# Query projection fed by activations ahead of their normalisation, in a one-layer hybrid decoder step

## The reference, cut to what matters

```python
def rmsnorm(x, g):
    xf = x.astype(F32)
    y = xf * lax.rsqrt(jnp.mean(jnp.square(xf), axis=-1, keepdims=True) + NORM_EPS)
    return (y * g.astype(F32)).astype(x.dtype)

def mem_attn(h, mk, mv, w_mq, w_mo):
    q = (h @ w_mq).reshape(B, T, MEM_HEADS, MEM_HEAD_DIM)
    s = jnp.einsum('bthd,bmhd->bhtm', q, mk) * (MEM_HEAD_DIM ** -0.5)
    p = jax.nn.softmax(s, axis=-1)
    o = jnp.einsum('bhtm,bmhd->bthd', p, mv).reshape(B, T, D_MODEL)
    return o.astype(h.dtype) @ w_mo

    # in layer():
    x = x + jnp.concatenate([a, b], axis=-1).astype(x.dtype) @ w_out
    x = x + mem_attn(rmsnorm(x, norm_mem_g), mk, mv, w_mq, w_mo)
    x = x + peer(rmsnorm(x, norm_ffn_g), peer_wq, peer_subkeys, peer_u, peer_v)
```

## Time and profile before

| what | value |
|---|---|
| median of 3 runs | 4757.11 us (4755.58 to 4757.85) |
| the profiled execution | 4756.82 us, its span 4754.9 us |
| mean granted TensorE clock | 0.969 of full speed |
| PE busy | 4437.2 us, 93% |
| POOL busy | 3059.0 us, 64% |
| DVE busy | 2364.5 us, 50% |
| ACT busy | 1561.5 us, 33% |

### The profile page before, as it was taken

One profiled execution on the slowest core, in us unless ns is written; L12 is line 12 of the kernel. 1 busy time (PEld: TensorE's weight loads), 2 busy tenths in 40 slices (PEclk: granted clock), 3 DMA queues, 4 the chain that ended last, 5 costly groups with the idle time before them and its releaser, 6 DMA issues.

```text
span 4754.9 us, 75671 instructions
## 1 busy us (share of the span) xinstructions
PE 4437.2 (93%) x28747; PEld 4178.8 (88%) x28747; DVE 2364.5 (50%) x3080; ACT 1561.5 (33%) x1954; POOL 3059.0 (64%) x1558
## 2 busy tenths in 40 slices
PE   7999999898998989999999887999999999999997
PEld 7799999797887978888888787999999999999997
DVE  3622333313002165555555554666666666667656
ACT  4422222212222244444444443333333333333333
POOL 6833322232222457777777665899999899998864
PEclk9999999999998999999999888999999999999998
DMA  6643333423654255555555457899999999999964
GB/s 219 199 87 105 108 108 108 146 81 111 218 197 153 93 164 184 182 184 185 186 183 183 139 152 230 330 341 345 344 343 347 327 343 340 348 344 357 335 194 136
DMA packets 556785, 1031.87 MB, mean 217 GB/s; under 512 B 137073, under 2 KB 342001, under 8 KB 523889
## 3 DMA queue, kind: packets, MB, share of 16 engines
q1 hardware_dynamic: 314384, 590.67, 38.2%
q0 software_dynamic: 45056, 268.60, 14.4%
q10 hardware_dynamic: 197216, 170.85, 11.0%
HBM read 935.26 MB, written 94.73 MB: 217 GB/s over the span
## 4 chain that ended last, share of the span: by engine, by line
PE 37%; issue 26%; POOL 26%; DMA 4%; DVE 3%; another core or an unknown queue 2%; ACT 1%; ACTq 0%; POOLq 0%; DVEq 0%; SPq 0%
POOL WS L424 21%; PE PS L811 15%; PE PS L529 12%; PE PS L879 9%; POOL ROWS L458 3%; DMA AR<-in_vE 2%; POOL AR L448 2%; PE PS L854 1%; DMA RAW<-in_vE 1%; ACT WS L911 1%; DVE AR L1427 1%; DVE AR L1401 1%; DMA gel<-AR 0%; POOL AR L458 0%
## 5 line engine op out<-in xcount | busy, mean ns | idle before, releaser
L529 PE MATMUL PS<-HL,WS 128*128 128x288 f32 (+2 forms) x16896 | 2421.9, 304 | 122.1 <-DVE HL L1438 33.8
L529 PEld LDWEIGHTS PS<-HL,WS 128*128 128x128 f32 x16896 | 2367.5, 191 | 153.1 <-issue 102.4
L424 POOL TENSOR_TENSOR WS<-RAW,WS 128x1024 fp32r<-128x1024 f32 x602 | 1477.1, 2466 | 1296.0 <-ACT WS L911 1291.3
L879 PE MATMUL PS<-WW,WS 128*128 128x320 f32 x6144 | 940.8, 315 | 80.5 <-POOL WS L424 65.3
L879 PEld LDWEIGHTS PS<-WW,WS 128*128 128x128 f32 x6144 | 921.1, 192 | 99.5 <-issue 81.9
L911 ACT ACTIVATE WS<-RAW 128x1024 fp32r<-128x1024 f32 x602 | 617.8, 1055 | 994.9 <-PE PS L529 351.0
L811 PE MATMUL PS<-WS,HL 128*128 128x512 f32 x3072 | 700.1, 389 | 0.0
L811 PEld LDWEIGHTS PS<-WS,HL 128*128 128x128 f32 x3072 | 575.6, 188 | 118.9
L424 POOL TENSOR_TENSOR WS<-AR,WS 128x1024 fp32r<-128x1024 f32 x238 | 600.4, 2526 | 45.8 <-ACT WS L911 44.8
L424 POOL TENSOR_TENSOR WS<-CS,WS 128x1024 fp32r<-128x1024 f32 x200 | 492.5, 2462 | 199.7 <-ACT WS L911 198.1
L1714 DVE SCALAR_TENSOR_TENSOR PS<-ROWS,AR,PS 128x2048 f32<-128x2048 f32 x206 | 483.8, 2348 | 73.2 <-DMA ROWS<-in_vE,AR 72.9
(11 more groups left out here) (163 smaller groups left out, 2308.1 us busy)
## 6 DMA issues: line engine op xcount, KB each, us to landing
RAW<-in_uT SPq DMA_DIRECT2D x256, 512.0 KB
RAW<-in_w_lin SPq DMA_DIRECT2D x218, 512.0 KB
CS<-in_uT SPq DMA_DIRECT2D x128, 512.0 KB
AR<-in_uT SPq DMA_DIRECT2D x128, 512.0 KB
RAW<-in_vE SPq DMA_DIRECT2D x128, 512.0 KB
CS<-in_vE SPq DMA_DIRECT2D x64, 512.0 KB
AR<-in_vE SPq DMA_DIRECT2D x64, 512.0 KB
AR<-in_w_lin SPq DMA_DIRECT2D x46, 512.0 KB
```

Of the source, the lines that this page charges most:

```text
L424: pool.tensor_tensor(WS[:, k, 1, :], raw(k, many, late), WS[:, k, 0, :].bitcast(F32), ALU.subtract)\
L529: ins = mm(to, WS[:, slot + hf, wp, k * P:(k + 1) * P], x, start=first and (wp, xp) == (0, 0), stop=last and wp == 1, skip_group_check=True)
L879: ins = mm(bank(2 + d % 2, ND), WS[:, 2 * (q % 2) + b, vp, 512 * e + P * d4:512 * e + P * (d4 + 1)], W[:, 2 * b + e, wp, :], start=(b, e, ...
```

## The change

Three things are done.

1. The activations of the queries are split without the per-token factor: the high part is `X` times the gain, made by ACT in one instruction (L1192 of the new text), and the low part is `X` times gain minus the high part, in one DVE instruction (`gained_low`). Blocks 0 to 14 of `HL` are overwritten while PE works on output block 15, each as soon as PE has read the old block (`hl_free`). Block 15 follows when it has been added.
2. The sum of squares for the factor is taken by PE within `query(0, 0)`, after its tenth input block (`sum_within`). DVE makes the factor `RSTD`, and multiplies each query block by it when it takes it out of PSUM (`evac_queries`), for all four heads. ACT no longer evacuates queries. Queries are linear in the normalised activations, so the result is the same in exact arithmetic.
3. `X` is stored to `x2T` in four pieces, three of them during the output projection. SP loads the keys of head 0 after slice `H_MQ + 7` in place of `H_MQ + 11`, and waits for `RSTD` ahead of them. Buffers move to make room for `RSTD`.

```diff
-            load_lin(H_RET, H_MQ + 12)
+            load_lin(H_RET, H_MQ + 8)
             sp.wait_ge(S["lo_ready"], LO_MQ + 16)
-            sp.wait_ge(S["out_x"], 16)
+            sp.wait_ge(S["out_x"], 64)
+            sp.wait_ge(S["rstd_ready"], 1)
...
             load_keys(0)
+            load_lin(H_MQ + 8, H_MQ + 12)
...
                         if kb in marks:
                             ins.then_inc(S["used"], 1)
+                        elif frees:
+                            ins.then_inc(S[frees], 1)
...
-            norm_sum(2)
...
+            def sum_within(k2):
+                if k2 == 4:
+                    norm_sum(2)
             for m in range(4):
-                query(0, m)
+                query(0, m, sum_within if m == 0 else None)
...
-            add_stage(2, H_OUT, B_OUT)
-            act.dma_start(x2T.rearrange("k p t -> p k t"), X).then_inc(S["out_x"], 16)
+            for b in range(KB - 1):
+                act.wait_ge(S["used"], used(H_OUT + 2 * b + 2))
+                high2(H_OUT + 2 * b + 4, 2 * (b % 2))
+                if b:
+                    act.wait_ge(S["lin_evac"], B_OUT + b + 2)
+                    square(2, b - 1, X)
+                if b % 4 == 0 and b:
+                    act.dma_start(x2T[b - 4:b].rearrange("k p t -> p k t"), X[:, b - 4:b, :]).then_inc(S["out_x"], 16)
+            for b in range(KB):
+                if b == 7:
+                    act.wait_ge(S["used"], used(H_OUT + 2 * KB - 1))
+                elif b < KB - 1:
+                    act.wait_ge(S["hl_free"], b + (b < 7))
+                else:
+                    act.wait_ge(S["lin_evac"], B_OUT + KB + 2)
+                    square(2, KB - 1, X)
+                act.activation(HL[:, 0, b, :], X[:, b, :], ACT.Identity, scale=GAINS[:, G_MEM + b:G_MEM + b + 1])\
+                    .then_inc(S["hi_ready"], 1)
+                if b == 2:
+                    act.wait_ge(S["lin_evac"], B_OUT + KB + 1)
+                    square(2, KB - 2, X)
+            act.dma_start(x2T[KB - 4:KB].rearrange("k p t -> p k t"), X[:, KB - 4:KB, :]).then_inc(S["out_x"], 16)
+            act.wait_ge(S["used"], used(H_OUT + 2 * KB))
+            high2(H_OUT + 2 * KB + 2, 2)
             root(2)
-            for b in range(KB):
-                high_part(48, b)
...
-                copy(halves(QM[:, m, :]), pair(m % 2)).then_inc(S["lin_evac"], 1)
...
-            add_residual(2, H_OUT)
-            rstd(2, summed=True)
-            normed(X, G_MEM, LO_MQ)
+            def gained_low(b):
+                dve.wait_ge(S["hi_ready"], LO_MQ + b + 1)
+                stt(HL[:, 1, b, :], X[:, b, :], GAINS[:, G_MEM + b:G_MEM + b + 1], HL[:, 0, b, :].bitcast(F32),
+                    ALU.mult, ALU.subtract).then_inc(S["lo_ready"], 1)
+            for n in range(KB - 1):
+                add_block(2, H_OUT, n)
+                if n:
+                    add_square(2, n - 1)
+            for b in range(KB - 1):
+                gained_low(b)
+                if b == 2:
+                    add_square(2, KB - 2)
+            add_block(2, H_OUT, KB - 1)
+            add_square(2, KB - 1)
+            gained_low(KB - 1)
+            dve.wait_ge(S["sum_done"], 3)
+            ts(halves(NVAR), pair(3), EPS, None, ALU.add).then_inc(S["var_ready"], 1)
...
+            newton(NRS, NVAR, NACC, RSTD)
+            dve.sem_inc(S["rstd_ready"], 1)
             link(dve.memset(AR[:, 2304:3840], 0.0))
+            def evac_queries(h):
+                for m in range(4):
+                    dve.wait_ge(S["used"], h * 8 + used(H_MQ + 2 * m + 2))
+                    tt(halves(QM[:, m, :]), pair(m % 2), halves(RSTD), ALU.mult).then_inc(S["lin_evac"], 1)
+            evac_queries(0)
```

More of the change, by code:

```diff
@@ L239, in build @@
         INZ, OSR = ar(19408, 4, 32), ar(19536, RD)
[L241 to L244, removed]
+        QM, QZ, PTZ, RSTD = ar(0, 4, T), ar(2304, SB, 4, 32), ar(3328, 2, 2, 4, 32), ar(3840, T)
+        KT, VT, KVS = ar(4416, 4, MEM), ar(5440, 2, MD), ar(6464, SB, 2 * MD)
+        PR, PT, OB, OSB = ar(14656, TILES, MEM), ar(15936, 2, TP), ar(16960, 4, T), ar(14656, MD)
+        MX, NMX, SM, RSM = ar(19264, TILES), ar(19269, TILES), ar(19274, TILES), ar(19279, TILES)
         Z_OUT = (CS[:, 0, :], CS[:, 1, :], RAWQ[:, 4, :])
-        Z_MO = (CS[:, 0, :], CS[:, 1, :], ar(19220, T))
+        Z_MO = (CS[:, 0, :], CS[:, 1, :], ar(19284, T))
         QP, SC, SV = ar(0, 2, RT5), ar(1280, 2, TILES, NK), ar(2560, 2, TILES, TOPK)
@@ L507, in projection @@
             def projection(n, m, a, slot, moving=both_halves, ready=None, between=None,
-                           part=(0, KB), marks=(KB // 2 - 1, KB - 1), first_bank=None):
+                           part=(0, KB), marks=(KB // 2 - 1, KB - 1), first_bank=None, frees=None):
                 if part[0] == 0:
@@ L594, in out_early, with out_rest @@
                            marks=(KB // 2 - 1,) if m == 0 else (), between=between)
-            def out_rest(first, block, early, lo):
+            def out_rest(first, block, early, lo, frees=None):
                 for m, marks in ((0, (KB - 1,)), (1, (KB - 2, KB - 1))):
                     projection(first + 2 * m, block + m, m, 2 * m, ready=lo, part=(early, KB), marks=marks)
-                with pe.Fori(0, 7) as i:
+                with pe.Fori(0, 6) as i:
                     for s in range(2):
                         projection(i * 4 + (first + 4 + 2 * s), i * 2 + (block + 2 + s), s, 2 * s)
+                for b in (KB - 2, KB - 1):
+                    projection(first + 2 * b, block + b, b % 2, 2 * (b % 2), frees=frees if b == KB - 1 else None)
             def head_block(h, m, between=None):
@@ L715, in _, with query @@
             out_early(H_OUT, B_OUT, 1, OUT_EARLY, LO_OUT)
-            out_rest(H_OUT, B_OUT, OUT_EARLY, LO_OUT)
-            norm_sum(2)
-            def query(h, m):
-                projection(h * 8 + (H_MQ + 2 * m), h * 4 + (B_MQ + m), m % 2, 2 * (m % 2), ready=LO_MQ)
+            out_rest(H_OUT, B_OUT, OUT_EARLY, LO_OUT, frees="hl_free")
+            def query(h, m, between=None):
+                projection(h * 8 + (H_MQ + 2 * m), h * 4 + (B_MQ + m), m % 2, 2 * (m % 2), ready=LO_MQ, between=between)
             def attention(h, more):
@@ L1234, in _ @@
             for b in range(KB):
-                high_part_peer(64, b)
+                high_part_peer(48, b)
             act.wait_ge(S["lo_ready"], LO_FFN + 16)
@@ L1380, in _ @@
             for b, end in ((0, 4), (4, 8), (8, 12), (12, 14), (14, 16)):
-                act.wait_ge(S["t_ready"], 80 + end)
+                act.wait_ge(S["t_ready"], 64 + end)
                 act.dma_start(yT[b:end].rearrange("k p t -> p k t"), X[:, b:end, :]).then_inc(S["out_y"], 16)
@@ L1557, in _, with add_block @@
             dve.sem_inc(S["rvar_ready"], 1)
+            def add_block(k, first, n):
+                dve.wait_ge(S["used"], used(first + 2 * n + 2))
+                if n % 4 == 0:
+                    dve.wait_ge(S[f"in_x{n // 4}"], 16 * k)
+                tt(halves(X[:, n, :]), halves(X[:, n, :]), pair(n % 2), ALU.add).then_inc(S["lin_evac"], 1)
             def add_residual(k, first):
                 for n in range(KB):
[L1562 to L1565, removed]
+                    add_block(k, first, n)
                     if n:
@@ L1596, in attention @@
                 dve.sem_inc(S["p_done"], 1)
+                if more:
+                    evac_queries(h + 1)
             with step.loop(MH - 1, 3) as h:
```

15 lines of the change are left out of this document (8 added, 7 removed).

## The result

The changed kernel takes 4723.39 us (median of 4 runs, 4717.47 to 4724.72) against 4756.34 us of the kernel before (4 runs, 4755.15 to 4757.85). The ratio is 0.9928, its 95% interval 0.9911 to 0.9945, so it is faster by 26 to 42 us. 4725.8 was forecast.

What follows compares the result with a forecast made beforehand. PE was taken to bound the kernel, busy 93% of the span. Gains of 27.4 (pause) and 4.3 (keys) less 0.4 (evacuation) make 31.3 us, forecasting 4725.8 us; own range 4722 to 4729, range asked for 4720 to 4735.

Steps and rivals of the forecast that it cites:

- The pause: Between output block 15 and the end of the first query block: PE's idle and slow query go, 27.4 us gained.
- the tightest place: Norm's sum within the first query block: PE wants it at 1116.7, ready at 1116.9; 0.2 us of wait taken.
- The step that made the first low part late: During output block 15, POOL's weight work holds up DVE's first low part, which ends 0.6 us after POOL, at 1102.9.
- The value for the evacuation: DVE's evacuation of each head's fourth query block: 0.76 us against ACT's 0.65, 0.4 us lost over four heads.
- its upper bound of 2 us: If POOL holds up DVE's evacuations, up to 2 us for each of four, 8 us in all.
- The factor: Ahead of the first evacuation: ready at 1126.3, or about 1131 if POOL holds DVE up; needed at 1135.6, cost 0.
- The keys: Scores of head 0: earlier key loads remove PE's wait and slower matmuls around it, 4.28 us gained.
- A: DVE is held up in the first query block and at four evacuations; 10 us given back, about 4735; chance 0.10.
- C: The first query block cannot start until block 15's add; PE waits 9 us, 4735, or 4756 with whole pause; chance 0.03.
- B: The keys' gain in head 0 does not come; 4.3 us missing, 4730; chance 0.08.
- D: Slower: without the pause PE is granted less clock in the rest of the span; 4770 at 1% less; chance 0.03.
- the untouched stages: All behind the queries moves ahead as a whole; only the last head could shift by itself, 2 us either way.

Runs made afterwards that it cites:

- keys_only: The kernel before with only the keys of head 0 loaded after slice H_MQ + 7; 4688.9 us, ratio 0.9989.
- before_values_late: The kernel before, with the last head's cached values issued only when the 12 early low parts are made; 4680.78 us, ratio 0.9969.
- after_again: The changed kernel run again with no edit; 4662.88 us, ratio 0.9930 to the kernel before.
- after_third: The changed kernel run a third time with no edit; 4660.97 us, ratio 0.9926 to the kernel before.
- sum_at_once: The changed kernel with the norm's sum put back ahead of the first query block; 4674.64 us, ratio 0.9956 to the kernel before.
- split_after_block: The changed kernel with high and low parts made only after output block 15 has ended; 4667.7 us, ratio 0.9941 to the kernel before.
- keys_back: The changed kernel with the keys of head 0 loaded behind slice H_MQ + 11 again; 4665.7 us, ratio 0.9943 to the kernel before.
- values_late: The changed kernel, with the last head's cached values issued only when the 12 early low parts are made; 4648.66 us, ratio 0.9911.

## Why the prediction was right

**The pause.** 27.4 us were worked out, 27.48 came (with the 0.1 us of the evacuation in it), and 27.50 on the first and on the third chip of the experiments (80.54 in `keys_only` and in `before_values_late`, which stand up to there as the kernel before does, less 53.04 in `after_again` and `after_third`). The sum within the block was busy for 1.13 us, for 1.05 in the prediction, and the tightest place held: I had the last square added at 1116.9 for a wish of PE at 1116.7; it was added by 1114.20 in a profile that lies 1.83 earlier, so by 1116.0 on the old scale. I had taken 0.78 us for each low part from two L1427; twelve took 0.74 each. `sum_at_once` and `split_after_block` split the gain: 10.5 us hang on the place of the sum, 3.8 on the overlap. That `X` is stored in four pieces has no run of its own.

**POOL.** The step that made the first low part late was right: 4.42 us for three where 2.2 would do, and its end 0.6 us behind POOL, as taken. The value for the evacuation was right too (0.93 us of idle for 0.82), and its upper bound of 2 us is refuted as contention, but not as a price: behind the 3.03 us of idle that a late evacuation made, the granted clock was 0.58. The factor was ready at 1128.15, 1130.0 on the old scale, by the late one of the two times in the prediction (1131), since POOL did hold up two of the instructions that make it; PE did not wait for it.

**The keys.** 4.28 us were forecast, 4.18 came in head 0, together with 0.1 for the evacuation; `keys_only` and `keys_back` show it from both sides.

**The rivals.** A and C would have shown as waits of PE at L531 between output block 15 and the scores of head 0, and there is none; A's other part, a late evacuation, would have shown as more idle than 0.93 us before the scores. A's sum in the prediction adds 4 us where its sentence says 3. B is refuted by 10.7 us in head 0. D would have shown in the clock: the mean grant rose from 0.969 to 0.972.

**Where the size was not mine.** The total came 2.4 us better than the forecast for the profiled execution (33.7 for 31.3, by 4756.82 and 4723.16), but that is not the sum of its terms. I gave the untouched stages 2 us either way, in head 3 alone. They moved by 1.8, 3.1, 4.5 and 8.2 us in both directions, and that they left only -2.5 is luck: without the 8.2 us of the rest alone the profiled execution would have been at 4731, outside the forecast's own range of 4722 to 4729. For head 3 the cause of its length is shown: the values. Among kernels in which the values are not held back it varies from 69.0 to 76.9 us. That loads beside each other come out otherwise each time would fit, but no kernel shows what sets the draw. For the output blocks a cause is not settled (below). The 8.2 us of the rest, 3085.06 and 3076.88, stay open as well: in the experiments the rest spans 3014.6 to 3022.3 over all kernels, and 3 us between two profiles of one text, so most of such a spread needs no change.

## What to carry to other kernels

A per-row factor of a norm need not stand in front of the matmuls: multiply it in where the product leaves PSUM, and the chain of sum, root and reciprocal has a whole block to hide under; then place the small reduction where its operand is sure to be ready, since four matmuls in the wrong place cost 10.5 us here. When one engine sets the end, price a pause with what the clock does behind it: here 2.7 us of wait were worth 4.3, and 2.1 us more idle in front of the scores made them 2.9 us longer. And before believing a few microseconds of a total, lay both profiles out by stretches: a third of what moved here lay in stages that nobody had changed.

## What was not expected

The 15 output blocks behind the attention run at 12.48 us a block in some executions and at 12.80 in others, 130.0 or 133.3 ns a matmul, at a granted clock of 1.00 in both. One kernel (`values_late`) showed 12.48 in one profile and 12.80 in the next, so it is not the program text that decides. It is worth 4.5 us. The output blocks ahead of the attention had 12.80 in every profile. What sets the pace was not found.
